# Reordering the start of a two-block transformer kernel: weight chunks staged in idle memory, and the first projection cut into halves

## The reference, cut to what matters

```python
mod_l = (silu(c)    @ ada_w[0] + ada_b[0])      # 1024 x 6144, one row
mod_c = (silu(c_ctx) @ ada_w[0] + ada_b[0])
sh1, sc1, ... = split(mod, 6)
rms(x, g)  = x * rsqrt(mean(x*x) + 1e-6) * g
a_l = rms(x,   norm_mix[0]) * (1 + sc1_l) + sh1_l
a_c = rms(ctx, norm_mix[0]) * (1 + sc1_c) + sh1_c
qkv = a @ na_w_qkv[0]                           # 1024 x 3072, both sides
```

## Time and profile before

| | |
|---|---|
| median of 3 runs | 1690.48 us (1689.5 to 1691.49) |
| the profiled execution | 1688.79 us |
| its span (first to last instruction) | 1687.6 us, 25828 instructions |
| PE / PE weight loads / DVE / ACT busy | 95% / 84% / 54% / 40% of the span |
| loaded from HBM | 248.55 MB, 148 GB/s over the span |

### The profile page before, as it was taken

How to read it: one execution, slowest core, us unless ns; L and a number is a source line. 1 busy time by engine, 2 the same in 40 slices (tenths; PEclk the granted TensorE clock), 3 DMA queues, 4 the chain that set the end, 5 groups by cost and what they waited for, 6 DMA issues and landing times.

```text
span 1687.6 us, 25828 instructions
## 1 busy us (share of the span) xinstructions
PE 1608.8 (95%) x11251; PEld 1412.5 (84%) x11251; DVE 906.3 (54%) x1199; ACT 680.5 (40%) x917; POOL 81.7 (5%) x124
## 2 busy tenths in 40 slices
PE   5899999989999999989898999987999999999998
PEld 3678866767777778878668999987999999899998
DVE  4522277463243333356766555547677755477763
ACT  2411266342221221235564444433455445354452
POOL 4000043000000000000000000005000000000000
PEclk7799999999999999999898999998999999899999
DMA  9754542335554542243103555545455464455552
GB/s 254 236 195 151 175 36 23 119 107 200 174 185 165 174 150 94 81 149 124 53 2 103 197 176 170 183 156 172 150 176 185 160 205 150 135 181 184 178 178 70
DMA packets 242977, 251.27 MB, mean 149 GB/s; under 512 B 4797, under 2 KB 240672, under 8 KB 242864
## 3 DMA queue, kind: packets, MB, share of 16 engines
q1 hardware_dynamic: 240112, 244.34, 44.5%
q0 software_dynamic: 2464, 5.09, 2.6%
q10 hardware_dynamic: 288, 0.19, 0.0%
HBM read 248.55 MB, written 1.05 MB: 148 GB/s over the span
## 4 chain that ended last, share of the span: by engine, by line
PE 91%; DVE 4%; DMA 2%; ACT 1%; issue 1%; SPq 0%; DVEq 0%; ACTq 0%
PE psum L318 88%; PE psum L732 2%; DMA raw<-in_ada_w 2%; DVE wl L302 1%; DVE sums L795 1%; DVE pt L809 1%; ACT wh L295 0%; DMA raw<-in_na_w_qkv 0%; DVE acc L957 0%; DVE acc L1406 0%; ACT scr L762 0%; DVE hT L965 0%; DVE proj L1690 0%; DVE xl L458 0%; DVE scr L448 0%
## 5 line engine op out<-in xcount | busy, mean ns | idle before, releaser
L318 PE MATMUL psum<-xh,wh 128*128 128x256 f32 (+1 forms) x1936 | 620.7, 321 | 8.3 <-DVE wl L302 4.9
L318 PE MATMUL psum<-xl,wh 128*128 128x256 f32 (+1 forms) x1936 | 613.4, 317 | 0.0
L318 PE MATMUL psum<-xh,wl 128*128 128x256 f32 (+1 forms) x1936 | 612.5, 316 | 0.0
L302 DVE TENSOR_TENSOR wl<-raw,wh 128x2048 fp32r<-128x2048 f32 (+1 forms) x186 | 418.2, 2250 | 316.8 <-ACT wh L295 316.6
L295 ACT ACTIVATE wh<-raw 128x2048 fp32r<-128x2048 f32 (+1 forms) x186 | 347.9, 1874 | 401.7 <-PE psum L318 396.1
L318 PEld LDWEIGHTS psum<-xh,wh 128*128 128x128 f32 x1936 | 374.8, 194 | 48.4 <-issue 13.9
L318 PEld LDWEIGHTS psum<-xh,wl 128*128 128x128 f32 x1936 | 374.4, 193 | 22.7
L318 PEld LDWEIGHTS psum<-xl,wh 128*128 128x128 f32 x1936 | 374.9, 194 | 21.3 <-issue 0.5
L318 PE MATMUL psum<-ah,wh 128*128 128x256 f32 (+1 forms) x704 | 218.6, 310 | 0.0
L318 PE MATMUL psum<-al,wh 128*128 128x256 f32 (+1 forms) x704 | 218.1, 310 | 0.0
L318 PE MATMUL psum<-ah,wl 128*128 128x256 f32 (+1 forms) x704 | 217.9, 310 | 0.0
(11 more groups left out here) (239 smaller groups left out, 1612.4 us busy)
## 6 DMA issues: line engine op xcount, KB each, us to landing
raw<-in_ada_w SPq DMA_DIRECT2D x48, 1024.0 KB, 5.1
raw<-in_ffn_w_in SPq DMA_DIRECT2D x44, 1024.0 KB, 5.0
raw<-in_w_ffn_gate SPq DMA_DIRECT2D x22, 1024.0 KB, 5.1
raw<-in_w_ffn_up SPq DMA_DIRECT2D x22, 1024.0 KB, 5.1
raw<-in_ffn_w_out SPq DMA_DIRECT2D x16, 1024.0 KB, 5.0
raw<-in_w_ffn_down SPq DMA_DIRECT2D x16, 1024.0 KB, 5.0
raw<-in_na_w_qkv SPq DMA_DIRECT2D x12, 1024.0 KB, 5.3
raw<-in_w_in_even SPq DMA_DIRECT2D x8, 1024.0 KB, 5.6
```

The source lines that it names most:

```text
L302: dve.e.tensor_tensor(wl[:, c % NSPL, 0:z], raw[:, p % NRAW, 0:z], wh[:, c % NSPL, 0:z].bitcast(F32), ALU.subtract).then_inc(W.lo, 1)
L318: return pe.e.matmul(o, l, r, start=start, stop=stop, skip_group_check=shared)
```

## The change

Nothing is computed differently but for the order of roundings. In the program:

- Four `ada` chunks go to tiles of their own, `pre[0..3]`, in memory that is idle until q and k are written, and a fifth, `pre[4]`, to another idle place. SP issues the first four without any wait right after x and ctx, then the projection chunks 0 and 1, then `pre[4]`, and only then `ada` 5, 6, 7 through the ring.
- The first eight `ada` chunks are two batches of four. The order is (shift 0, 1, scale 0, 1), (shift 2, 3, scale 2, 3).
- DVE copies the even groups f to `hT`, ACT the odd ones.
- When 1/rms is spread, DVE makes `hn` = x / rms for all rows k. After a batch, a row takes two one-source DVE operations (`tensor_scalar`, hn x coef + shift), one ACT copy to `xh0` and one DVE subtraction to `xl0`, the last two over 512 columns at once.
- `qkv0_first_pe`: chunk 0 rows 0 to 3; `ada` 4 to 7; chunk 1 rows 0 and 1; fold; chunk 1 rows 2, 3; chunk 0 rows 4 to 7; `ada`; chunk 1 rows 4 to 7; `ada`.
- POOL's 15 small loads wait for x and ctx, and the first two groups of the attention bias wait until PE has turned the small vectors, behind chunk 1.

```diff
-        ADA = [(0, i) for i in (0, 4, 1, 5, 2, 6, 3, 7)] + [(0, i) for i in range(8, 24)] + [(1, i) for i in range(24)]
-        BATCHES = [[a] for a in range(8)] + [range(8, 20), range(20, 24), range(24, 36), range(36, 48)]
+        ADA = [(0, i) for i in (0, 1, 4, 5, 2, 3, 6, 7)] + [(0, i) for i in range(8, 24)] + [(1, i) for i in range(24)]
+        BATCHES = [range(0, 4), range(4, 8), range(8, 20), range(20, 24), range(24, 36), range(36, 48)]
...
-        dma = [("ada", a) for a in range(8)]
-        for c in range(NW):
+        dma = [("w", 0), ("w", 1), ("ada", 5), ("ada", 6), ("ada", 7)]
+        for c in range(2, NW):
...
+            for a in range(4):
+                sp.e.dma_start(view(pre[a], 0, ada_src(a)), ada_src(a)[0]).then_inc(s_pre[a], 16)
             for p, (kind, x) in enumerate(dma):
+                if p == 2:
+                    sp.wait_ge(C.vt, 1)
+                    sp.e.dma_start(view(pre[4], 0, ada_src(4)), ada_src(4)[0]).then_inc(s_pre[4], 16)
...
-            for a in range(8):
-                if a:
-                    ada_fold(a - 1)
-                ada_mm(a)
...
+            ada_mm(0)
+            pe.wait_ge(X.sum, KT)
+            stat_pe(0, 4)
+            ada_mm(1)
+            spread_pe(0, 4)
+            ada_mm(2)
+            ada_mm(3)
+            ada_fold(0)
...
+            split_hi(0)
+            split_hi(1)
             act.wait_ge(X.sum, KT)
             for k in range(KT):
-                if k == 4:
-                    split_hi(0)
-                normed_act(0, TT, 0, 0, xh0, k)
+                act.wait_ge(N.scaled, 2 * k + 2)
+                act.e.activation(xh0[:, k, :], scr[:, k % 6, :], ACT.Copy).then_inc(N.xh, 2)
...
+            for k in range(KT):
+                dve.e.tensor_tensor(hn[:, k, :], hT[:, k, :], stat[:, :], ALU.mult).then_inc(X.hn, 1)
...
+            ada_copy(0)
+            split_lo(0)
+            ada_add(0)
+            first_coefs(0)
+            for k in range(4):
+                first_normed(k)
+            first_low(3)
+            split_lo(1)
+            ada_copy(1)
+            ada_add(1)
+            first_coefs(1)
+            for k in range(4, 8):
+                first_normed(k)
+            first_low(7)
...
+            part(0, range(4))
+            for a in range(4, 8):
+                ada_mm(a)
+            part(1, range(2))
+            ada_fold(1)
+            part(1, range(2, 4))
+            part(0, range(4, 8)).then_inc(W.used, 1)
+            ada_pe(0)
+            part(1, range(4, 8)).then_inc(W.used, 1)
+            ada_pe(1)
...
         def gpsimd_program():
+            pool.wait_ge(L.x, 32)
             for dst, src in rest_loads:
                 pool.e.dma_start(dst, src).then_inc(L.rest, 16)
+            pool.wait_ge(C.turned, 2)
             bias_pool(0)
```

More of the change, by code:

```diff
@@ L484, in program @@
         C = semaphores(nc, "c", "turned vt act dve")
-        X = semaphores(nc, "x", "turned hT square sum")
+        X = semaphores(nc, "x", "turned hT_d hT_a square sum hn")
         cf = ins["conv_ffn_2"].rearrange("l k (m p) -> (l k m) p", p=P)
@@ L585, in setup_dve @@
             add_square(KT - 1)
[L587 to L595, removed]
@@ L613, in setup_dve @@
-            ada_add(7)
-            for k in (6, 7):
-                normed_dve(0, TT, 0, 0, xh0, xl0, k, first_coef)
-            normed_low(0, TT, 0, 0, xh0, xl0, 15)
-            dve.wait_ge(L.rest, NREST)
-            dve.wait_ge(C.vt, 2)
-            dve.e.tensor_tensor(small[:, 44:52], vcol(V_NFIN, 8), vcol(V_NMIX2, 8), ALU.mult)
-            dve.e.tensor_scalar(gain[:, 0:1], gain[:, 0:1], 0.125, None, ALU.mult).then_inc(C.dve, 1)
+            recip_dve(0, 4)
+            diag_dve(0, 4)
@@ new lines, in setup_dve, with first_coefs @@
+            dve.wait_ge(N.spread, 1)
+            dve.wait_ge(X.turned, KT)
+            dve.wait_ge(X.hT_a, KT // 2)
+            for k in range(KT):
+                dve.e.tensor_tensor(hn[:, k, :], hT[:, k, :], stat[:, :], ALU.mult).then_inc(X.hn, 1)
+            def first_coefs(b):
+                w = slice(4 * b, 4 * b + 4)
+                dve.wait_ge(A.mod, b + 1)
+                for s in range(2):
+                    dve.e.scalar_tensor_tensor(coef[:, 0, 0, s, w], mod[:, 0, 8 + 4 * b:12 + 4 * b, s], 1.0, vcol(V_NMIX + 4 * b, 4),
+                                               ALU.add, ALU.mult).then_inc(N.coef, 2)
+                dve.wait_ge(N.coef, 4 * b + 4)
@@ new lines, in first_low, with first_normed @@
+            def first_low(k):
+                dve.wait_ge(N.xh, 2 * k + 2)
+                dve.e.tensor_tensor(xl0[:, k, :], scr[:, k % 6, :], xh0[:, k, :].bitcast(F32), ALU.subtract).then_inc(N.xl, 2)
+            def first_normed(k):
+                dve.wait_ge(X.hn, k + 1)
+                if k >= 6:
+                    dve.wait_ge(N.xl, 2 * (k - 6) + 2)
+                for s in range(2):
+                    w = slice(s * T, s * T + T)
+                    dve.e.tensor_scalar(scr[:, k % 6, w], hn[:, k, w], coef[:, 0, 0, s, k:k + 1], mod_col(0, 0, k, s), ALU.mult,
+                                        ALU.add).then_inc(N.scaled, 1)
+                if k % 4:
+                    first_low(k - 1)
@@ L648, in program, with qkv0_first_pe, part @@
         Q0 = semaphores(nc, "qkv0", "act dve")
+        def qkv0_first_pe():
+            out_ = bank[0:2], bank[2:4]
+            def part(c, ks):
+                h, l = taken(c)
+                for k in ks:
+                    pe.wait_ge(N.xl, 2 * k + 2)
+                    for m in range(2):
+                        w = slice(m * P, (m + 1) * P)
+                        last = three(out_[c][m][:, :], h[:, k, w], l[:, k, w], xh0[:, k, :], xl0[:, k, :], k == 0, k == KT - 1)
+                return last
+            part(0, range(4))
[8 more added lines that the diff above has]
+            ada_pe(1)
+            pe.wait_ge(L.rest, NREST)
+            for g in range(2):
+                last = pe.e.transpose(bank[6][:, g * P:(g + 1) * P], vrow[:, g + 1, :], ident)
+            last.then_inc(C.turned, 1)
         def qkv0_pe():
-            for step in st_qkv0:
+            qkv0_first_pe()
+            for step in st_qkv0[2:]:
                 i = step[1]
@@ L682, in qkv0_act, with rest_dve @@
                         split_pair_hi(0, j)
+        def rest_dve():
+            dve.wait_ge(C.turned, 2)
+            dve.e.tensor_copy(vt[:, P:384], bank[6][:, 0:2 * P]).then_inc(C.vt, 1)
+            dve.wait_ge(C.vt, 2)
+            dve.e.tensor_tensor(small[:, 44:52], vcol(V_NFIN, 8), vcol(V_NMIX2, 8), ALU.mult)
+            dve.wait_ge(L.rest, NREST)
+            dve.e.tensor_scalar(gain[:, 0:1], gain[:, 0:1], 0.125, None, ALU.mult).then_inc(C.dve, 1)
         def qkv0_dve():
```

104 lines of the change are left out of this document (45 added, 59 removed).

## The result

The changed kernel took **1674.49 us** (median of 4 runs, 1670.29 to 1676.08), the kernel before in the same comparison 1690.82 us: ratio 0.9901, 95% interval 0.9879 to 0.9922. The profiled execution took 1672.93 us, with a span of 1671.7 us against 1687.6. The forecast of the time was right to a tenth of a microsecond, closer than the runs agree among themselves (they lie 5.8 us apart), but not each step was: the mark, the first matmul of chunk 2, stands at 67.94 us, 14.2 us earlier than before and not 16.1, and the rest of the gain came where I had expected nothing.

A forecast was written before the change was run, and what follows sets the result against it. PE bounds 91% of the chain, but loads bound the first 55 us. Chunk 2 starting 16.1 us earlier takes 1688.79 to 1672.7; adding 1.7 for the median gives 1674.5 us, range 1671.5 to 1678.

The forecast's parts named there:

- Start of the transposes: PE's first transposes start at 9.3 us instead of 10.27, taking 1.0 us for small loads moved behind x and ctx.
- Sum ready: Turning, squaring and summing on DVE and ACT, at 1.8 us per pair of groups, finish at 18.65 us.
- Spread done: 1/rms takes 2.7 us after the sum and its spread on PE 1.5, ending at 22.9 us.
- Chunk 0: First projection chunk lands at 26.5 us: 5.9 MB queued, 24.6 at 382 GB/s, 37.4 at 209.
- First matmul of chunk 0 (S): After chunk 0's split and the first norm rows, PE starts on chunk 0 at 33.9 us; range 32.5 to 36.5.
- From S to the mark: PE's interleaved rows and `ada` steps take 32.2 us from chunk 0's first matmul to chunk 2's first matmul.
- Behind the mark: After chunk 2's first matmul the same matmuls follow in both kernels, so everything moves by the same amount.
- A: PE's clock falls between chunk 0's row halves, during `ada` 4 to 7: 2 to 5 us, 1676.5 to 1679.5; chance 0.15.
- B: Start loads stay slow because of vector loads: chunk 0 at 37.4, gain only 5 us, 1685.5; chance 0.11.
- C: Slower: the queue ahead of chunk 0 drains at 142 GB/s, 1698.7 us; break point chunk 0 at 45.5; chance 0.04.
- D: The gain is absorbed by another PE wait before the attention, time staying at 1690.5 us; chance 0.04.
- Edits at no cost: Bias groups moved to about 66 and 80 us, late small vectors and reused staging memory delay nothing.

The follow-up runs named there:

- run 9: The changed kernel with the 15 small loads issued at once instead of behind x and ctx: 1675.54 us, ratio 0.9909.
- run 6: The changed kernel with chunk 1's rows 0 to 3 moved from around the fold to behind chunk 0: 1676.0 us, one run.
- Run 4: The changed kernel with `hn` made for rows 0 to 3 before the first batch, rows 4 to 7 behind chunk 1's split: 1671.78 us, ratio 0.9892.
- Run 2: The changed kernel with one attention bias group (four loads) put back ahead of the 15 small loads: 1677.43 us, one run.
- Runs 3: The changed kernel without the staging tiles, all eight first `ada` chunks going through the ring of three: 1677.8 us, ratio 0.9925.
- runs 1: The kernel before, with only the first two bias groups loaded later, behind the second projection chunk: 1682.94 us, ratio 0.9957.

## Why the prediction was right, step by step

- **Start of the transposes**: said 9.3, was 9.91. The term of 1.0 us for the small loads was mis-sized; run 9 measured 0.4.
- **Sum ready**: said 18.65, was 20.2. From the first transpose it took 10.3 us, where I had 9.35. The pair of groups is not 1.8 us: the chain has copy 0.61, square 0.64 and add 0.69 in series across two engines, 2.0 with the handovers. I had added up the busier engine's work and left the handovers out.
- **Spread done**: said 22.9, was 26.0; this is the step that failed most. From the sum on it took 5.8 us, not 4.2. The PE rows show why: the eight matmuls of the sum took 1.86, and `ada` 1, which PE's order puts between, 1.93, and the spread 2.08, all at half clock. I had left `ada` 1 out of the path. I had priced the clock in the spread alone (1.5) and taken the 2.7 before it from a stretch at full clock. That the clock fell near the start of the sum and not at its end is itself not given by the instructions: in run 6, with the same ones, the spread ended 0.9 us earlier.
- **Chunk 0**: said 26.5, was 25.0, so 382 GB/s was the rate and the margin I had added was not needed. It was reached because the small loads stood behind x and ctx, which I had priced for ctx alone: at once, they put chunk 0 at 26.6 (run 9). The Trainium skill's 358 GB/s (DMA: Bandwidth & Descriptors, Where 436 GB/s comes from) doesn't fit these windows of 380 to 399.
- **First matmul of chunk 0 (S)**: said 33.9, was 36.4, inside its range. What bound was `hn` and the split on DVE, which the text named only for the case of an early load; with the spread 3.1 us late and the load 1.5 us early that case was the one that came. Run 4 shows it: `hn` cut in half moves S by 2.2 us. Run 2 shows the other side: chunk 0 6.2 us late moves S by only 2.0.
- **From S to the mark**: said 32.2, was 31.5. Rows 0 to 3 took 7.6 (7.4), the clock was back at S + 4 and stayed, `ada` 7 was asked for at 41.95 and landed 5.03 us later with 0.18 us of wait (said: S + 10.4, less than 1 us of wait; was S + 10.6). Each part is right within 0.7 us.
- **The mark**: said 66.1, was 67.94, so 1.8 us of the expected 16.1 did not come.
- **Behind the mark**: said to be the same, was 1.6 us shorter (1603.8 against 1605.4 us), 1.5 of it in the one stretch shown above. That this made up for the missing 1.8 us is luck: the forecast of 1672.7 for the profiled execution met 1672.93 through two errors of opposite sign. The 1.7 us that I added for the median is a difference between runs that scatter more than that, so the last digits of the median are luck as well. With the mark as it was and an unchanged rest, the profiled execution would have taken 1688.79 - 14.2 = 1674.6 us, and the forecast would have been 1.9 us too low, still inside its range.
- **The rivals.** A came in another place than I had put it: the clock fell at 21 us, not at 46. Runs 3 and 6 show that it does come at 46 to 51 us as soon as PE waits 2 to 3 us there. B's forecast fell with chunk 0 at 25.0, and C's with it; runs 1 and 2 show the bias loads as the cause of the two slowest windows, and run 9 leaves B a true part, the window from 12 to 15 us, worth 1.6 us at chunk 0. (C's sum was also off: chunk 0 at 45.5 and the other terms put the mark at 85.1, which is 2.9 us later than before and not 3.4.) D is out by the result: PE's next piece of 123.43 us stands directly behind, as the 150.62 did.
- **Edits at no cost**: the bias loads, now issued from 68 to 86 us, landed in 9.7 us at most, and no PE wait names them.

## What to carry to other kernels

When a wait for loads is removed at the start, write down the chain of arithmetic that is next with its handovers and with PE at half clock, since it bounds as soon as the data comes early. Small loads can cost a weight stream far more than their bytes, as the four bias loads with overlapping short rows did here, and the 15 vector loads issued at once to a lesser degree: put them where the stream has slack. And with scatter of a clock behind it, judge an edit of 1 to 3 us by a mark in the profile right behind the edit, not by the total alone; and compare each piece up to the mark, since here the mark itself moved by 0.9 us without an edit.

## What the runs showed that I had not expected

**Issuing a load can take microseconds.** SP's queue in the changed kernel (start, us, line, what):

```profile
2.03 0.47 SPq L275 DMA_DIRECT2D vtok<-in_ctx  x1
2.54 10.15 SPq L277 DMA_DIRECT2D pre<-in_ada_w  x4
12.73 6.23 SPq L290 DMA_DIRECT2D raw<-in_na_w_qkv  x2
19.01 3.32 SPq L281 DMA_DIRECT2D pre<-in_ada_w  x1
```

Where one issue takes 0.28 to 0.58 us otherwise, each of the seven behind the first chunk's (`ada` 1 to 3, `w` 0 and 1, `ada` 4 and 5) took 2.6 to 3.5 us, about the time in which 1 MB moves at this rate (1.049 MB at 382 GB/s is 2.7 us). With x, ctx and one chunk outstanding the next issue is held, it seems until the queue has moved on. It cost nothing here, as the stream stayed full, but the loads behind it are issued late: "without any wait" in the code was not so on the queue.

**Bias rows.** One group of four loads, 0.39 MB in overlapping rows of 64 values, took the stream from 382 GB/s to 250 and then 152, over 3 us each, and delayed chunk 0 by 6.2 us (run 2), where 0.39 MB at full rate is 1.0 us.

**The clock's response is not a function of the instructions.** The same idle piece of 0.91 us was followed by half clock in eight profiles and not in five, at 1.5 us each time.
